# Splitting the post-norm residual update of the last sub-layer over VectorE, ScalarE and GpSimd

## The reference, cut to what matters

```
def rmsnorm(x, g):
    y = xf * lax.rsqrt(jnp.mean(xf * xf, axis=-1, keepdims=True) + RMS_EPS)
    return y * g
...
def swiglu_ffn(h, w_gate, w_up, w_down):
    g = jnp.einsum("bsd,df->bsf", h, w_gate)
    u = jnp.einsum("bsd,df->bsf", h, w_up)
    return jnp.einsum("bsf,fd->bsd", jax.nn.silu(g) * u, w_down)
...
x = x + rmsnorm(parallel_conv_mixer(rmsnorm(x, mix_pre_g), ...), mix_post_g)
x = x + rmsnorm(memory_cross_attention(rmsnorm(x, xa_pre_g), ...), xa_post_g)
x = x + rmsnorm(swiglu_ffn(rmsnorm(x, ffn_pre_g), w_gate, w_up, w_down), ffn_post_g)
```

## Time and profile before

| what | value |
|---|---|
| median of 2 runs | 1151.53 us (1141.92 and 1161.15) |
| the profiled execution's own time | 1141.22 us |
| its span, slowest core (core 6) | 1139.6 us; the other cores 1123.5 to 1138.6 |
| granted TensorE clock, mean by core | 0.973 to 0.982 of full speed |
| TensorE matmuls busy | 1030.0 us, 90% of the span |
| VectorE, ScalarE, GpSimd busy | 370.1 us (32%), 447.8 us (39%), 266.7 us (23%) |

### The profile page before, as it was taken

One profiled execution on the slowest core, in us unless ns is written; L12 is line 12 of the kernel. 1 busy time (PEld: TensorE's weight loads), 2 busy tenths in 40 slices (PEclk: granted clock), 3 DMA queues, 4 the chain that ended last, 5 costly groups with the idle time before them and its releaser, 6 DMA issues.

```text
span 1139.6 us, 24968 instructions; the slowest of 8 cores (1123.5 to 1139.6 us)
## 1 busy us (share of the span) xinstructions
PE 1030.0 (90%) x9136; PEld 883.3 (78%) x9136; DVE 370.1 (32%) x852; ACT 447.8 (39%) x1045; POOL 266.7 (23%) x425
## 2 busy tenths in 40 slices
PE   1899999999999788999997799999999999999993
PEld 1788788787887664888785688888888888888883
DVE  8233333432433421444444022222221222222212
ACT  2244354444443634656663224242423324142311
POOL 3002021020221312113254323131312323232321
PEclk9899999999999988999998899999999999999997
DMA  9970000000000985910037977767677676676671
GB/s 157 185 224 2 1 2 1 2 1 2 1 2 26 164 145 88 162 21 1 1 43 71 131 107 125 102 97 129 91 134 109 118 105 122 97 130 98 120 108 44
DMA packets 73480, 93.14 MB, mean 82 GB/s; under 512 B 26352, under 2 KB 41968, under 8 KB 73232
## 3 DMA queue, kind: packets, MB, share of 16 engines
q0 software_dynamic: 58320, 75.64, 45.8%
q1 hardware_dynamic: 15040, 15.90, 4.7%
HBM read 156.54 MB, written 8.39 MB: 145 GB/s over the span
## 4 chain that ended last, share of the span: by engine, by line
PE 78%; DMA 6%; ACT 5%; issue 4%; DVE 3%; POOL 2%; DVEq 0%; ACTq 0%; POOLq 0%
PE ps L385 46%; PE ps L794 13%; PE ps L526 10%; DMA t<-w_mix_in 3%; DMA t<-w_q 2%; PE ps L361 2%; ACT t L394 2%; POOL t L419 2%; DVE t L414 1%; PE ps L500 1%; DMA t<-w_down 1%; PE ps L399 1%; PE ps L701 1%; PE ps L721 1%; ACT L404 1%
## 5 line engine op out<-in xcount | busy, mean ns | idle before, releaser
L385 PE MATMUL ps<-t,t 128*128 128x256 bf16 (+1 forms) x5824 | 689.7, 274 | 29.1 <-DMA t<-w_mix_in 11.5
L385 PEld LDWEIGHTS ps<-t,t 128*128 128x128 bf16 x5824 | 564.9, 99 | 108.3 <-issue 35.0
L419 POOL TENSOR_TENSOR t<-t,t 128x256 f32<-128x256 f32 x188 | 132.1, 726 | 464.0 <-ACT t L355 276.9
L794 PE MATMUL ps<-t,t 128*128 128x256 bf16 x1408 | 183.3, 274 | 13.4 <-DMA t<-w_down 7.0
L847 ACT ACTIVATE t<-ps 128x256 f32<-128x256 f32 x176 | 67.3, 386 | 309.2 <-PE ps L385 284.9
L850 DVE TENSOR_TENSOR t<-ps,t 128x256 bf16<-128x256 f32 x176 | 73.8, 423 | 350.4 <-ACT t L847 344.7
L345 POOL DMA_DIRECT2D t<-w_down x176 | 93.5, 534 | 306.4 <-PE ps L794 297.3
L794 PEld LDWEIGHTS ps<-t,t 128*128 128x128 bf16 x1408 | 137.7, 98 | 34.3 <-issue 17.8
L414 DVE SCALAR_TENSOR_TENSOR t<-ps,t,t 128x256 f32<-128x256 f32 x192 | 88.6, 482 | 189.8 <-ACT t L406 153.1
L526 PE MATMUL ps<-t,t 128*128 128x256 bf16 x992 | 111.3, 272 | 0.0
L394 ACT ACTIVATE t<-ps 128x256 bf16<-128x256 f32 x192 | 67.5, 393 | 102.8 <-PE ps L385 77.0
(11 more groups left out here) (70 smaller groups left out, 495.3 us busy)
## 6 DMA issues: line engine op xcount, KB each, us to landing
t<-w_down POOLq DMA_DIRECT2D x176, 256.0 KB, 5.0
outT<-t SPq DMA_DIRECT2D x7, 1024.0 KB, 9.1
t<-xT SPq DMA_DIRECT2D x6, 1024.0 KB, 18.6
t<-w_gate POOLq DMA_DIRECT2D x2, 2816.0 KB, 30.8
t<-w_up POOLq DMA_DIRECT2D x22, 256.0 KB, 14.9
t<-w_mix_in POOLq DMA_DIRECT2D x4, 1024.0 KB, 23.7
t<-xT POOLq DMA_DIRECT2D x2, 1024.0 KB, 26.4
t<-w_mix_out POOLq DMA_DIRECT2D x2, 1024.0 KB, 52.1
```

The costliest lines, as they stand in the source:

```text
L385: S.op("pe", (lambda kc=kc: lambda e: e.matmul(hb(dst_bank, dst_half, n), lhsT=lhs_fn(kc), rhs=rhs_fn(kc), start=(kc == 0), stop=(kc == nk ...
L419: S.op("dve" if (last and oc % 2 == 1) else "pool", (lambda oc=oc, xs=xs: lambda e: e.tensor_tensor(out=xs(), in0=xs(), in1=tb[:, oc % nt, ...
L794: S.op("pe", (lambda oc=oc, b=b, hf=hf, slot=slot, j=j: lambda e: e.matmul(hb(b, hf), lhsT=wd_slot_cols(slot, oc * 128, (oc + 1) * 128), r ...
```

## The change

In phase 3 `PN` is replaced by `PN_split`. It goes over four pairs of chunks. The first of a pair (0, 4, 1, 5) goes as before: DVE multiplies by gain and `rstd_post`, POOL adds to x (in the last tile DVE adds). The second (2, 6, 3, 7) is read from PSUM by ACT, with a Copy whose scale is the gain; POOL multiplies it by `rstd_post` in place and then adds it to x. DVE has scratch buffers 0 and 1, ACT has 2 and 3. Phases 1 and 2 keep `PN`.

```diff
+        def PN_split(t, norm, tb, last=False):
+            S.cur = "PN"
+            dve_ocs = (0, 4, 1, 5)
+            act_ocs = (2, 6, 3, 7)
+            for i in range(4):
+                oc = dve_ocs[i]
+                b, hf = ybank(oc)
+                S.op("dve", (lambda oc=oc, b=b, hf=hf, i=i: lambda e: e.scalar_tensor_tensor(
+                    out=tb[:, i % 2, :], in0=hb(b, hf), scalar=gcol(norm, oc), in1=rstd_post[:, :],
+                    op0=ALU.mult, op1=ALU.mult))(),
+                    reads=["small", "rstd_post"], writes=["tmp%d" % (i % 2), bk(b)])
+                xs = lambda oc=oc: x_sb[:, oc, t * TT:(t + 1) * TT]
+                S.op("dve" if last else "pool", (lambda xs=xs, i=i: lambda e: e.tensor_tensor(
+                    out=xs(), in0=xs(), in1=tb[:, i % 2, :], op=ALU.add))(),
+                    reads=["tmp%d" % (i % 2)], writes=["x%d_%d" % (oc, t)])
+                oc = act_ocs[i]
+                b, hf = ybank(oc)
+                sl = 2 + i % 2
+                S.op("act", (lambda oc=oc, b=b, hf=hf, sl=sl: lambda e: e.activation(
+                    out=tb[:, sl, :], in_=hb(b, hf), func=AF.Copy, scale=gcol(norm, oc)))(),
+                    reads=["small"], writes=["tmp%d" % sl, bk(b)])
+                S.op("pool", (lambda sl=sl: lambda e: e.tensor_tensor(
+                    out=tb[:, sl, :], in0=tb[:, sl, :], in1=rstd_post[:, :], op=ALU.mult))(),
+                    reads=["tmp%d" % sl, "rstd_post"], writes=["tmp%d" % sl])
+                xs2 = lambda oc=oc: x_sb[:, oc, t * TT:(t + 1) * TT]
+                S.op("pool", (lambda xs2=xs2, sl=sl: lambda e: e.tensor_tensor(
+                    out=xs2(), in0=xs2(), in1=tb[:, sl, :], op=ALU.add))(),
+                    reads=["tmp%d" % sl], writes=["x%d_%d" % (oc, t)])
...
-                PN(t, 5, tbuf=tmp4, nt=4, last=last)
+                PN_split(t, 5, tmp4, last=last)
```

## The result

The changed kernel takes 1184.8 us (median of 11 runs, the lowest 1181.7); beside it the kernel before took 1141.6 us (median of 10). The ratio is 1.037, with a 95% interval from 1.036 to 1.039: slower, by some 43 us. Single runs of both kernels lie far higher (up to 1231 and 1266 us), with a lower granted clock on one die; the ratio leaves them out. The forecast was 1178 us, in a range of 1163 to 1196.

What follows compares the result with a forecast made beforehand. TensorE's waits at phase 3's seven tile boundaries, and the end, were taken to decide. 7 x (3.5 us of waiting + 1.7 of clock) + 0.5 for the end = 36.9 us on 1141.2 gives 1178 us, range 1163 to 1196.

Steps and rivals of the forecast that it cites:

- What bounds the kernel: TensorE's waits at phase 3's seven tile boundaries, and the end, decide; a boundary costs 1.41 us of waiting, seven 9.9 us.
- POOL and DVE: At a boundary, POOL starts an operation every 0.69 us, a dependent addition 0.93 us after its multiplication; DVE's reads wait for buffers.
- ACT: At each boundary, late Copies hold the table load and Silu of GU(1), so GU(4) starts 3.5 us later.
- The table load: Between the fourth Copy and the Silu at each boundary: 1.30 us in all, the load of 1.28, not 2.66.
- Rival E: The table switch costs 1.28 us more behind the Copies at each of seven boundaries: 1187 us, chance 0.08.
- The clock: TensorE's granted clock drops after the gap at each boundary, costing 1.7 us, with bounds 0 and about 3.4.
- 0.50 for some 3 us after it: Expected sign at each boundary of phase 3: the granted clock is 0.50 for some 3 us after GU(4) starts.
- The end: Last tile's post-norm: DVE and POOL additions hold each other up, +0.5 us, between 0 and 1.7.
- POOL's DMA queue: Loads of w_down behind the post-norm are issued up to 3.8 us later; needed over 18 us later, so no cost.
- B: The 8 matmuls inside each boundary's gap keep the clock up: 1166 us, chance 0.12.
- C: The table load goes ahead of the Copies, GU(4) 2.65 us later per boundary: 1172 us, chance 0.05.
- D: ACT reads banks 2 and 3 early, so each boundary's 1.41 us wait vanishes: 1131 us or part of it, chance 0.05.

Runs made afterwards that it cites:

- e6: Kernel before, with eight own scratch buffers, ACT reading only bank 3's two chunks and DVE the other six (0, 4, 1, 5, 2, 6): 1135.7 us, ratio 0.995.
- e2: Changed kernel with ACT's third and fourth Copy, and POOL's work from there on, moved behind the Silu of GU(2): 1166.0 us, ratio 1.022.
- e1: Changed kernel with four more scratch buffers, so each of the eight chunks has its own: 1137.9 us, ratio 0.997.
- e4: Changed kernel with 33 spare matmuls that nobody needs in TensorE's waits at each boundary: 1167.3 us, ratio 1.023.
- e8: e6 with only DVE's read order changed, to chunks 0, 1, 2, 4, 5, 6: 1132.3 us, ratio 0.992 to the kernel before.
- e7: Kernel before, without the split, with two scratch buffers instead of four in phase 3: 1165.8 us, ratio 1.021.

## Why the prediction was right, point by point

**What bounds the kernel.** The boundaries: between the first and the last Ln of phase 3 lie 41.06 us, and what differs outside (-0.70 and +0.74) cancels.

**POOL and DVE.** Right in mechanism, both small prices off. The dependent addition starts 0.86 us after the multiplication (764.53 to 765.39), for which I took 0.93. DVE's second read starts at 763.87, 0.66 us after the first and not 0.40, for the reason found in e6. It cost nothing here, since the third read waits for POOL anyway.

**ACT.** Right, with the order of the events as forecast: the fourth Copy starts 5.45 us after the Exp ends (forecast 5.5 to 6, so just under it), the table load directly behind it, and GU(4) is released by the product. The term was +3.5 us a boundary, measured +3.43 at six of them and +3.76 at the first. A Copy takes 0.47 us, as taken from L404. That the two waits lie one behind the other is shown by e2, that the buffers start it by e1.

**The table load.** The row held: from the end of the fourth Copy (768.96) to the Silu (770.28) are 1.32 us, though the Copies stand ahead of it. Rival E, one load more, is excluded, and with it here the figure of 2.66 us in the Trainium skill ("ScalarE: Activation LUTs", What ACT_TABLE_LOAD costs).

**The clock.** Right that it falls at each boundary, wrong in size: +1.7 us forecast, +2.4 measured, the term of the sum that was too small and that makes 1178 too low. I had charged the loss of the row at 626.11, where the low stretch took a GU and a down. Here the 16 matmuls of GU(4) took 3.37 us, down(1) 1.71 and GU(5) 1.95 instead of 1.74, 0.87 and 1.74: 2.68 us at this boundary. The slow stretch was twice as long: from 770.1 to 776.9, 6.8 us, against 3.4 at 626.11 (626.7 to 630.1). It began over a microsecond ahead of GU(4) and outlasted GU(4) and down(1), so that the sign "0.50 for some 3 us after it" fell short too: it was over 5. Six of the seven boundaries are so; at the one of the shortest tile (66.5 us) the clock was low for 3.4 us only, and 1.3 us were lost. The others take 67.15 to 68.05 us. Why it was mostly twice as long is not shown. The loss lies within the bound I had given (up to 3.4). The sum was short by 4.3 us (36.9 against 1182.4 - 1141.2 = 41.2): 16.7 - 11.9 = 4.8 of the clock and 0.2 of the end, less 0.2 for the term of ACT (24.3 against 24.5) and the 0.7 of the earlier work, and 0.2 of rounding.

**The end.** +0.5 us forecast, +0.74 measured, of which 0.42 are up to the last addition (8.32 us after the Ln starts, before 7.90) and the rest is the transfer of x behind it. DVE's and POOL's operations hold each other up as assumed, but mostly the other way round. DVE's first addition started behind a multiplication of POOL's and took 0.75 us; its other three started ahead of POOL's next operation and took 0.43, and POOL's took 0.78 to 0.96:

```profile
1168.51 0.75 DVE L421 TENSOR_TENSOR t<-t,t 128x256 f32<-128x256 f32 x1
...
1169.76 0.43 DVE L421 TENSOR_TENSOR t<-t,t 128x256 f32<-128x256 f32 x1
1169.81 0.96 POOL L430 TENSOR_TENSOR t<-t,t 128x256 f32<-128x256 f32 x1
```

**POOL's DMA queue.** The load of w_down behind the post-norm is issued at 772.75, 1.35 us after GU(4), and no wait for w_down follows it. Nothing, as forecast.

**The rivals.** B, the clock holds: e4 shows what it would have been, 1167 us, and its number was 1166. C: the load is behind the Copies. D, the relief is real: it is, once nothing waits for POOL; e8 takes about the 9.9 us of that rival, 9.7 by its trace and 9.0 by the ratio. In the changed kernel the relief was there for DVE (four reads) and was not worth anything, since two of them waited for POOL up to 1.75 us.

## What to carry to other kernels

When a stage is split over several engines, count the buffers between them first. A producer that runs through its list faster than its consumer needs enough of them to get to the end of it (here eight buffers for eight reads gained 6 us, and two instead of four cost 24), and a producer that waits for a buffer holds everything behind it in its list, here a table load, a Silu and through them TensorE. Ask of an engine that is given work what stands behind that work and who waits for it, not how busy it is. A longer wait of TensorE can cost again in the clock: here 3.4 us more of waiting cost 2.4 us of clock besides, the 1.8 us of e7 cost 1.6, and spare matmuls in the gap bought the clock's part back.

## What the runs showed of the hardware that was not expected

Thirty-three matmuls at each boundary whose results nobody reads made the kernel some 16 us faster, with the clock at 1.00 (2.4 GHz) from the first boundary to the last down. The clock also fell where no single wait was long: in e7 TensorE waited 1.07, 0.43, 0.61 and 0.42 us with a matmul between each, and it was at 0.50 behind them. At 1.2 GHz a load of weights and a matmul of 256 columns take 0.21 us from start to start, at 2.4 GHz 0.109. Of a DVE addition of two SBUF inputs and a POOL operation that overlap, in the last tile the one that started first kept its length (0.43 and 0.72 us) and the other took longer (DVE's 0.75, POOL's 0.78 to 0.96).
